# The output product in two column halves, the second half of its weights split later

## The reference

```
h    = rmsnorm(x) @ w_in                        # queries, keys, values, gates of three head groups
o_*  = the three attentions (sparse, retention, memory)
mix  = concat(o_n * silu(z_n), o_r * silu(z_r), o_m * silu(z_m))
x    = x + mix @ w_out                          # w_out is 1024 x 1024
y    = rmsnorm(x, ln_final)                     # for prompt and sample tokens
```

## Time and profile before

| | |
|---|---|
| median of 3 runs | 939.9 us (939.66 to 943.08) |
| profiled execution, its own time | 939.63 us |
| its span, first to last instruction | 937.8 us |
| PE busy | 895.2 us (95%) |
| DVE, ACT, POOL busy | 524.2, 413.7, 291.0 us |
| granted TensorE clock, mean | 0.999 |

### The profile page before, as it was taken

How to read it: one execution, slowest core, us unless ns; L and a number is a source line. 1 busy time by engine, 2 the same in 40 slices (tenths; PEclk the granted TensorE clock), 3 DMA queues, 4 the chain that set the end, 5 groups by cost and what they waited for, 6 DMA issues and landing times.

```text
span 937.8 us, 20464 instructions
## 1 busy us (share of the span) xinstructions
PE 895.2 (95%) x7594; PEld 811.5 (87%) x7594; DVE 524.2 (56%) x1501; ACT 413.7 (44%) x1063; POOL 291.0 (31%) x495
## 2 busy tenths in 40 slices
PE   6899999999999999999999999899999999999997
PEld 6899999999999899999988787768877787778885
DVE  4557332322323665645666787676777858844443
ACT  6434221224443011113466676565775667832221
POOL 0223212222223635435135153324422526410000
PEclk9999999999999999999999999999999999999999
DMA  7564414324240443231849058714604142343331
GB/s 230 156 206 136 151 45 152 103 88 121 67 145 25 132 142 98 95 105 63 219 132 284 4 160 264 255 57 119 181 2 131 56 141 77 102 137 133 128 121 67
DMA packets 85220, 117.91 MB, mean 126 GB/s; under 512 B 12930, under 2 KB 67506, under 8 KB 84546
## 3 DMA queue, kind: packets, MB, share of 16 engines
q1 hardware_dynamic: 71666, 73.12, 27.4%
q0 software_dynamic: 10224, 36.20, 11.5%
q10 hardware_dynamic: 3232, 7.28, 2.2%
HBM read 91.50 MB, written 32.02 MB: 132 GB/s over the span
## 4 chain that ended last, share of the span: by engine, by line
PE 78%; DVE 6%; issue 6%; ACT 5%; DMA 2%; POOL 2%; ACTq 0%; DVEq 0%; SPq 0%; POOLq 0%
PE psum L601 8%; PE psum L1866 7%; PE psum L602 7%; PE psum L603 7%; PE psum L1745 6%; PE psum L1722 4%; PE psum L1887 3%; PE psum L1886 3%; PE psum L1885 3%; PE psum L1723 3%; ACT p_P L1975 2%; PE psum L842 2%; PE psum L844 2%; PE psum L843 2%; PE psum L825 2%
## 5 line engine op out<-in xcount | busy, mean ns | idle before, releaser
L601 PE MATMUL psum<-a_whi,f_xhi 128*128 128x256 f32 (+1 forms) x672 | 194.7, 290 | 4.2 <-DVE a_hst L1127 2.6
L602 PE MATMUL psum<-a_wlo,f_xhi 128*128 128x256 f32 (+1 forms) x672 | 190.0, 283 | 0.0
L603 PE MATMUL psum<-a_whi,f_xlo 128*128 128x256 f32 (+1 forms) x672 | 189.6, 282 | 0.0
L1975 ACT ACTIVATE p_P<-psum,p_nb 128x640 f32<-128x640 f32 (+7 forms) x224 | 124.2, 561 | 45.8 <-DVE p_nb L2047 37.7
L601 PEld LDWEIGHTS psum<-a_whi,f_xhi 128*128 128x128 f32 x672 | 127.1, 189 | 6.9 <-DVE a_hst L1127 2.8
L602 PEld LDWEIGHTS psum<-a_wlo,f_xhi 128*128 128x128 f32 x672 | 127.2, 189 | 0.0
L603 PEld LDWEIGHTS psum<-a_whi,f_xlo 128*128 128x128 f32 x672 | 127.2, 189 | 0.0
L744 POOL DMA_DIRECT2D h_scratch<-a_hst x93 | 50.8, 548 | 211.7 <-DVE a_hst L1127 103.1
L1745 PE MATMUL psum<-f_ident,p_P 128*128 128x128 f32 x656 | 99.3, 275 | 1.4 <-ACT s_KTw L1925 0.7
L1745 PEld LDWEIGHTS psum<-f_ident,p_P 128*128 128x128 f32 x656 | 76.8, 140 | 8.0 <-DVE p_PT L1913 2.1
L2047 DVE CUSTOM_DVE_ANT_0 psum<-psum,p_near 128x256 f32<-128x256 f32 (+7 forms) x96 | 64.6, 673 | 31.2 <-PE psum L1723 25.3
(11 more groups left out here) (340 smaller groups left out, 2168.0 us busy)
## 6 DMA issues: line engine op xcount, KB each, us to landing
a_wraw<-in_w_in SPq DMA_DIRECT2D x24, 512.0 KB, 4.4
h_scratch<-a_hst POOLq DMA_DIRECT2D x72, 128.0 KB, 3.4
s_SG<-in_cache_nsa_slc SPq DMA_DIRECT2D x64, 128.0 KB, 2.3
p_qd<-q_scratch SPq DMA_DIRECT2D x16, 384.0 KB, 7.5
a_xraw<-in_x_prompt SPq DMA_DIRECT2D x8, 512.0 KB, 7.0
s_MK<-in_cache_mem SPq DMA_DIRECT2D x8, 512.0 KB, 8.6
s_WG<-in_cache_nsa_win SPq DMA_DIRECT2D x8, 512.0 KB, 5.3
mix_scratch<-p_zt POOLq DMA_DIRECT2D x8, 512.0 KB, 3.5
```

Source lines behind the costliest of these rows:

```text
L601: nc.tensor.matmul(out, hi, wh, start=first, stop=False)
L602: nc.tensor.matmul(out, hi, wl, start=False, stop=False)
L603: return nc.tensor.matmul(out, lo, wh, start=False, stop=last)
L1975: nc.scalar.activation(dst, s_view(s), ACT.Exp, bias=nb[:, g % NNB:g % NNB + 1], scale=1.0 if s[2] == 3 else -1.0, accum_out=ssum[:, par[i ...
```

## The change

The product of a tile is no longer one step but two, `("d", (d, half))`. The first products are put in a new order: tile 0 first half, tile 1 first half, tile 0 second half, turns of tile 2, tile 1 second half, turns of tile 3. From tile 2 on the two halves follow each other as before. The split's numbers 4 to 7 leave the groups beside the attention, which has eight groups fewer, and stand in the list behind the first half of tile 1. The first half of tile 0 waits for four subtractions of the split, the second for eight. `mm_rank` gives each half's place in the order of PE's halves, and the waits on `d_mm` use it.

```diff
--- before.py
+++ after.py
@@ -1414,8 +1414,8 @@
                        [("t", ("st", p, 3))], [("t", ("st", p, 0))], [("t", ("st", p, 1))], [("t", ("sv", p))] + ([("load_pair", p + 1)] if p + 1 < NPAIR else [("load_w", 0), ("load_w", 1)]),
                        [("store_pair", p)]]
         groups += [[("load_fin", 0)], [], [("fin", 0)], [], [], [], []]
-        for m in range(4):
-            groups += [[("w_hi", 2 * m)], [("w_lo", 2 * m)], [("w_hi", 2 * m + 1)], [("w_lo", 2 * m + 1)] + ([("load_w", m + 2)] if m < 2 else [])]
+        for m in range(2):
+            groups += [[("w_hi", 2 * m)], [("w_lo", 2 * m)], [("w_hi", 2 * m + 1)], [("w_lo", 2 * m + 1), ("load_w", m + 2)]]
         return groups
 
     def schedule():
@@ -1514,24 +1514,35 @@
                 for part in range(2):
                     add(("x", d, part))
         assert not groups, len(groups)
-        for d in range(NT):
-            steps.append(("d", d))
-            if d + 2 < NT:
-                steps.append(("load_m", d + 2))
-            if d == 0:
-                while waiting:
-                    pv()
-                while outs:
-                    write(outs.pop(0)[0])
+        def behind(d):
             if d + 2 < NT:
                 for part in range(2):
                     add(("x", d + 2, part))
             steps.append(("y", d))
             if d + 2 < NT:
                 steps.append(("load_x", d + 2))
+
+        steps.extend([("d", (0, 0)), ("load_m", 2)])
+        while waiting:
+            pv()
+        while outs:
+            write(outs.pop(0)[0])
+        steps.append(("d", (1, 0)))
+        for m in range(4, 8):
+            steps.extend([("w_hi", m), ("w_lo", m)])
+        steps.append(("d", (0, 1)))
+        behind(0)
+        steps.extend([("d", (1, 1)), ("load_m", 3)])
+        behind(1)
+        for d in range(2, NT):
+            steps.extend([("d", (d, 0)), ("d", (d, 1))])
+            if d + 2 < NT:
+                steps.append(("load_m", d + 2))
+            behind(d)
         return chunks, steps, act_of
 
     p_chunks, p_steps, p_act = schedule()
+    mm_rank = {dj: k + 1 for k, dj in enumerate(n for what, n in p_steps if what == "d")}
 
     def chunk_act(c):
 
@@ -1867,14 +1878,14 @@
                                             start=k == 0, stop=128 * (k + 1) >= keys, skip_group_check=True)
             i_mm.then_inc(S("p_pv"), 1)
 
-        def project(d):
+        def project(d, half):
             pe.wait_ge(S("pt_dve"), chunks_final_dve(x_last[d]))
             if d == 0:
-                pe.wait_ge(S("dw_split"), 8)
+                pe.wait_ge(S("dw_split"), 4 * half + 4)
                 pe.wait_ge(S("p_exp"), SM * QT)
             if d >= 2:
                 pe.wait_ge(S("d_sum"), 2 * (d - 1))
-            for jj in range(2):
+            for jj in (half,):
                 o = psum[:, 1024 * (d % 2) + 512 * jj:1024 * (d % 2) + 512 * jj + 512]
                 for k in range(KT):
                     if D_ORDER[d] == QT:
@@ -1897,7 +1908,7 @@
             elif what == "pv":
                 pv(n)
             elif what == "d":
-                project(n)
+                project(*n)
 
     def pt_copy(eng, copy, c, sem):
 
@@ -1981,7 +1992,7 @@
                     if kind[1] < 2:
                         act.wait_ge(S("p_qk"), NV)
                     else:
-                        act.wait_ge(S("d_mm"), 2 * (kind[1] - 1))
+                        act.wait_ge(S("d_mm"), mm_rank[kind[1] - 2, 1])
                     nc.scalar.copy(split_dst(n, False), split_src(n)).then_inc(S("p_shi"), 1)
                 elif chunk_act(n):
                     if kind[0] == "p":
@@ -2180,7 +2191,7 @@
                     dve.wait_ge(S("d_const"), 16)
                 v, v0 = small[0:r, 16 + n:17 + n], small[0:r, 96 + n:97 + n]
                 for jj in range(2):
-                    dve.wait_ge(S("d_mm"), 2 * n + jj + 1)
+                    dve.wait_ge(S("d_mm"), mm_rank[n, jj])
                     if jj == 0:
                         dve.wait_ge(S(f"d_x{n % 2}"), 16 * (n // 2 + 1))
                     o = 1024 * (n % 2) + 512 * jj
```

## The result

The changed kernel takes 943.54 us (median of 14 runs, 942.06 to 946.89) against 940.02 (14 runs of before, 937.53 to 943.77). The ratio is 1.0043, 95% interval 1.0028 to 1.0057: slower by 0.4%, inside the range that was given. The profiled execution took 944.51 us. Two executions in the later runs, of 2203 us (e7) and of 3273 us (e0b), are of a slow state and are left out of all ratios and medians.

A forecast was written before the change was run, and what follows sets the result against it. TensorE was taken as the bound, busy 895.2 of 937.8 us. Attention -0.9, late split +0.2 and late load +3.9 summed to +3.2 us: 939.6 to 942.8 us, 8-in-10 range 939.9 to 945.9.

The forecast's parts named there:

- The attention gains 0.9: End of the attention: taking four casts and four subtractions of the split out saves 0.9 us, bounds 0 and 2.3.
- The chain's 2.3 us for the cast: Chain of waits, 799 to 825.6 us: the split's cast has 8.6% of 26.6 us, taken as the gain's upper bound.
- the rival built on it: Attention gains all the chain shows: cast's 2.3 us and perhaps VectorE's 1.3 go, giving 940.8 us; chance 0.15.
- The split late, 0.2: Before tile 0's second half: PE waits 0.2 us for the moved split's subtractions, about 1.15 apart; bounds 0 and 1.9.
- The late load, 3.9: Before the turns of tile 3: PE waits 3.9 us once for load_m 3, queued behind load_x 2; only half a product covers it.
- The clock: Behind the wait for tile 3's load: the granted clock was forecast to stay at 1.00 throughout.
- the rival: TensorE's clock falls in the wait for tile 3's load, costing 1.7 us: 944.5, to 945.9; chance 0.23.
- The sum: Whole kernel: -0.9 + 0.2 + 3.9 = +3.2 us, from 939.6 to 942.8 us.

The follow-up runs named there:

- e7: Changed kernel, with the load of tile 3's rows also waiting until VectorE has ended tile 0; ratio to before 1.0103.
- e0b: The changed kernel run a third time, unaltered; ratio to before 1.0063.
- e2: Changed kernel with all eight split steps back beside the attention, only the new order of the halves kept; ratio to before 1.0049.
- e1: Changed kernel with the load of tile 3's rows put ahead of the load of tile 2's inputs in SP's queue; ratio to before 0.9990.
- e3: Changed kernel with products in the old order and the four late casts and subtractions right behind tile 0's first half; ratio to before 1.0000.
- e0: The changed kernel run again, unaltered; ratio to before 1.0070.
- e4b: Second run of e4, the changed kernel with 16 unused matmuls in front of the turns of tile 3; ratio to before 1.0052.
- e4: Changed kernel with 16 matmuls that nobody reads in front of the turns of tile 3; ratio to before 1.0054.
- e6: e1 with two late split pairs moved ahead of the last sums and the pairs beside the attention behind every second unit; ratio to before 0.9983.

## Why the prediction was right, step by step

- *The attention gains 0.9.* Measured 1.0 us in A (54.34 to 53.34), 0.9 in the repeats, and gone in e2. Most of it is idle time of PE in front of an exponential: such waits in A sum to 3.8 us before and 3.0 after; the wait of 1.02 us became 0.49 and that of 0.44 became 0.26. The rest, some 0.3 us, went from PE's listed busy time (50.95 to 50.68 us in A), so the reading that idle time alone comes back is not quite right: 0.11 us came from the block that had none. The chain's 2.3 us for the cast overstated the gain, and the rival built on it stayed away. Its own sum was wrong besides: 2.3 and 1.3 are 3.6 us, not the 2.9 that it took off.
- *The split late, 0.2.* It cost 0.7 in B (e1), 0.5 of it as a wait. The term that was too small is the pitch of the subtractions: 5.53 us for four, 1.38 apart, and not 1.15. They ran beside GpSimd's mixing, and both paid: subtractions of 1.21 to 1.76 us, and GpSimd operations of 1.33 us (128x128) and 1.72 (128x256), which take 0.47 and 0.75 in e3, where they don't meet. There the pitch is 1.16, the one that I had taken. I had read from one row that GpSimd alone pays. The rule of the Trainium skill ("SBUF — State Buffer", "SBUF: two separate sides"), that the two exclude each other on a shared port, agrees with this trace better than my reading did: 1.76 against 1.21 us.
- *The late load, 3.9.* Measured 3.83, 3.6, 3.7, 3.7. The chain was right term by term: 5.89 us from the turns to the issue (5.99 forecast, which counts from the weight load of the turns; from their matmul at 835.02 it is 5.88 before), and 4.4 us to the landing (4.3 forecast). e1 removes the wait with one exchange in the queue.
- *The clock.* I forecast that it stays, with a chance of 0.23 that it doesn't. It fell in three of four profiles (waits of 3.8, 3.7 and 3.7 us; not at 3.6). By my own list the forecast was wrong in this point: the rival took place in the profiled run, with the price that I gave it (1.7 us). That the price fits is luck: I had it from 4.2 us at a loss of 0.4, and the clock was low for 3.4 us at a loss of 0.5. My argument against it, that the gap was shorter than the 4.9 us after which the clock fell at the end of the kernel, took one observed delay for the least that is needed. The turns behind the wait, which I counted as some work, did not prevent it: in e2 and e0b the clock fell 0.5 and 0.9 us after they had begun. The advice of the Trainium skill ("TensorE: Matmul & The Clock Gate", "Why this matters for your kernels") against idle gaps speaks for the rival, and the trace agrees: 0.50 from 851 us on. It doesn't agree in every run: e0 kept 1.00 through a wait of 3.6 us.
- *The sum.* In the profiled run: -0.4 before A begins (scatter, as that stretch even has a fall of the clock near 307 us that before's profile has not), -1.0 in A, +0.7, +3.8 and +1.7 in B, together +4.8, against 4.88 measured between the two profiled executions (944.51 less 939.63). The forecast of +3.2 had the first and the last two in other sizes: 0.2 for 0.7, and 0 for 1.7. Over the 14 runs the difference of medians is 3.5 us, which is close to +3.2 in part by luck: the same terms give +3.5 without the fall and +5.2 with it, and the ratios of the changed kernel in the two later sets, 1.0070 and 1.0063, are 6.6 and 5.9 us.

## What to carry to other kernels

When work is reordered on one engine, follow every transfer queue through the new order: a load that had a whole product as cover had half of one, because it stood in the queue behind another load that waits for sums; an exchange of two queue entries was worth more than the whole change. Work taken off a helper engine gives back little more than the idle time of the bound engine that it caused: of 4.2 us of ACT's work 1.0 came back here. And an idle gap on TensorE like the ones of 3.6 to 3.8 us here is to be costed with the fall of its clock, as a matter of chance: three of four, at 1.7 us.

## What the runs showed of the hardware that I had not expected

The clock falls in several places of this kernel by chance, and that is probably much of the scatter between its runs. In the profiled run of the changed kernel it is also low from 307.6 to 311.0 us, 1.5 us behind the end of a wait of PE of 1.8 us that the kernel before has as well, without a fall. e0 and e4b show it at the same place, e2, e4 and e0b near 601, e3, e4b and e6 near 636, e4b near 484 as well. Each time it is low for some 3.4 us. The mean granted clock of a run goes with its time: of the runs of before in the first set of experiments, those at 0.998 took 937.5 to 938.5 us, those at 0.996 939.1 to 940.3, those at 0.994 940.3 to 941.5. Over all 62 runs of before beside the experiments these bands overlap (936.1 to 940.0, 938.1 to 941.2, 940.3 to 942.5), with means of 938.1, 939.6 and 941.3. The step of 0.004 from the first to the last is about two falls of 1.7 us, an estimate from the clocks; the one profile of before shows none. What decides whether it falls at a given place stays open.
